# Moving the delta rule's constants, low-rank inputs and first tiles, and the first cache pages, into the stages before them

## The reference, cut to what matters

```python
def _attend_paged(q_lat, q_pe, c_kv, k_pe, cache_ckv, cache_kpe, layer, page_table):
    def page_step(carry, pages):                     # 64 pages of 128 rows for each sample
        kc = cache_ckv[layer, pages]
        kp = cache_kpe[layer, pages]
        return _online(carry, _scores(q_lat, q_pe, kc, kp), kc), None
    carry, _ = lax.scan(page_step, init, page_table.T)
    ...                                              # then the sample's own 4 rows, masked

prev = jnp.concatenate([shift0[:, None].astype(rw.dtype), rw[:, :-1]], axis=1)
xr = rw + (prev - rw) * lw["rwkv_mu"]                # token shift, all RWKV columns
r, k, v, xw, xa, xg = jnp.split(xr, RWKV_SPLITS, axis=-1)
w = -jax.nn.softplus(-(lw["rwkv_w0"] + jnp.tanh(xw) @ lw["rwkv_w_up"])) - 0.5
a = jax.nn.sigmoid(lw["rwkv_a0"] + xa @ lw["rwkv_a_up"])
g = jax.nn.sigmoid(xg) @ lw["rwkv_g_up"]
S = S * wt[:, :, None, :] + sa[..., None] * bt[:, :, None, :] + vt[..., None] * kt[:, :, None, :]
new_shift = rw[:, -1]
```

## Time and profile before

| | us |
|---|---|
| median of 3 runs | 3769.72 (3756.41 to 3772.3) |
| the profiled execution | 3773.11, span of its instructions 3771.3 |
| PE busy | 3410.2 (90% of the span) |
| DVE / ACT / POOL busy | 1652.5 / 941.2 / 396.7 |
| prompt attention, first instruction to end | 1435.3 to 1623.9 |
| opening of sample attention, up to the first page's transpose | 1623.9 to 1646.0 |
| sample attention after that | 1646.0 to 2050.6 |
| masks, then low-rank inputs | 2050.6 to 2059.9 to 2075.9 |
| delta rule | 2075.9 to 2510 |

### The profile page before, as it was taken

One profiled execution on the slowest core, in us unless ns is written; L12 is line 12 of the kernel. 1 busy time (PEld: TensorE's weight loads), 2 busy tenths in 40 slices (PEclk: granted clock), 3 DMA queues, 4 the chain that ended last, 5 costly groups with the idle time before them and its releaser, 6 DMA issues. The chain is left out here.

```text
span 3771.3 us, 69383 instructions
## 1 busy us (share of the span) xinstructions
PE 3410.2 (90%) x28749; PEld 3049.2 (81%) x28749; DVE 1652.5 (44%) x2947; ACT 941.2 (25%) x1651; POOL 396.7 (11%) x452
## 2 busy tenths in 40 slices
PE   7999999979999799979996788869979999999877
PEld 6999999978999736756664576659969999999866
DVE  3343344353222144435453677755154343343454
ACT  3111111122000104534442334433141111111231
POOL 0000000010000000033330334420010000000112
PEclk9999999989999898989997799979989999999988
DMA  2111111113222300045553201014031111111032
GB/s 104 34 56 46 34 51 51 40 64 119 90 92 94 118 14 10 9 167 203 195 192 91 51 25 32 20 64 148 29 131 51 51 40 44 51 40 46 32 132 99
DMA packets 118755, 279.39 MB, mean 74 GB/s; under 512 B 46036, under 2 KB 57108, under 8 KB 117940
## 3 DMA queue, kind: packets, MB, share of 16 engines
q1 hardware_dynamic: 100052, 199.87, 15.7%
q0 software_dynamic: 18432, 75.51, 5.8%
HBM read 231.41 MB, written 43.80 MB: 73 GB/s over the span
## 5 line engine op out<-in xcount | busy, mean ns | idle before, releaser
L79 PE MATMUL f_psg<-f_u_hi,f_w_hi 128*128 128x352 f32 x1056 | 349.3, 331 | 49.5 <-DVE f_u_lo L359 24.0
L590 DVE TENSOR_TENSOR c_x<-c_x,f_psd 128x352 f32<-128x352 f32 x480 | 246.6, 520 | 318.3 <-PE f_psd L81 318.3
L79 PE MATMUL f_psd<-f_hid_hi,f_w_hi 128*128 128x352 f32 x1056 | 350.5, 332 | 18.2 <-DVE c_x L590 9.8
L475 ACT ACTIVATE f_w_hi<-f_raw 128x1024 fp32r<-128x1024 f32 x132 | 136.8, 1054 | 916.9 <-PE f_psd L81 352.0
L80 PE MATMUL f_psg<-f_u_lo,f_w_hi 128*128 128x352 f32 x1056 | 344.2, 326 | 0.0
L81 PE MATMUL f_psg<-f_u_hi,f_w_lo 128*128 128x352 f32 x1056 | 344.1, 326 | 0.0
L80 PE MATMUL f_psd<-f_hid_lo,f_w_hi 128*128 128x352 f32 x1056 | 341.7, 324 | 0.0
L79 PE MATMUL f_psu<-f_u_hi,f_w_hi 128*128 128x352 f32 x1056 | 341.4, 323 | 0.0
L81 PE MATMUL f_psd<-f_hid_hi,f_w_lo 128*128 128x352 f32 x1056 | 341.4, 323 | 0.0
L80 PE MATMUL f_psu<-f_u_lo,f_w_hi 128*128 128x352 f32 x1056 | 339.4, 321 | 0.0
L81 PE MATMUL f_psu<-f_u_hi,f_w_lo 128*128 128x352 f32 x1056 | 339.0, 321 | 0.0
(11 more groups left out here) (403 smaller groups left out, 7051.1 us busy)
## 6 DMA issues: line engine op xcount, KB each, us to landing
f_raw<-in_ffn_gu SPq DMA_DIRECT2D x88, 512.0 KB, 4.2
f_raw<-in_ffn_d SPq DMA_DIRECT2D x44, 512.0 KB, 4.1
proj<-in_out SPq DMA_DIRECT2D x36, 528.0 KB, 2.9
inw_raw<-in_w_in_units SPq DMA_DIRECT2D x36, 512.0 KB, 3.9
h<-c_x SPq DMA_DIRECT2D x24, 528.0 KB, 2.9
c_x<-proj SPq DMA_DIRECT2D x16, 528.0 KB, 4.3
mgw_raw<-in_merge_units SPq DMA_DIRECT2D x16, 512.0 KB, 4.7
plw_raw<-in_ple_units SPq DMA_DIRECT2D x8, 640.0 KB, 3.9
```

Of the source, the lines that this page charges most:

```text
L79: pe.matmul(out, w_hi, x_hi, start=start, stop=False)
L475: act.activation(w_hi[:, u % 3, :], raw[:, u % 3, :], ACT.Copy).then_inc(hi_done, 1)
L590: dve.tensor_tensor(a, a, ps_d[:, n % 2, 0:TB], ALU.add).then_inc(added, 1)
```

## The change

Three things are moved, and the buffers are laid out anew for it.

1. A class `SamplePages` owns the table, the row numbers, `q_block`, `q` and the four slots of `pages`. Its loads (`sp_loads`), the four row-number instructions (`dve_rows`, after the fourth item's maximum) and the first sample's whole gather (`pool_prepare`, `pool_sequence(pool, 0, 0, None, None)`: 4 groups, 16 indirect DMAs) run in prompt attention. Sample attention starts with 5 constants instead of 10, `own_t` first, and three clears instead of four.
2. A class `RwkvInputs` owns `lw`, `lg`, `starts`, `lora`, `par`, `padded`. Once `weighted` has reached `2 * NS` in sample attention, SyncE issues all of `load_constants`, `lora_phase` and the first loads of `rwkv_phase` (`sp_loads`), in that order: low-rank inputs, last rows, masks, constants, first three tiles, and the store of the shift rows. VectorE mixes the low-rank inputs (`dve_mix`) between the scaling of `acc` and the copy of `o_lat`. ScalarE's tanh and sigmoid (`act_gates`) follow its last body.
3. The phases `load_constants` (masks) and `lora_phase` are gone. `rwkv_phase` starts with the state's load.

`q_t` and `k_t` lie in tiles of 128 partitions (`queries`, `keys`), whose room `RwkvInputs` uses later. `acc`, `weights` and `uv` of sample attention lie in the room of `v`. The instructions of the loops are the same.

```diff
+class SamplePages:
+    def sp_loads(self, sp):
+        sp.dma_start(self.table[:, :], self.page_table.broadcast_to([P, DEC_BATCH * N_PAGES])).then_inc(self.table_in, 16)
+        for m in range(self.QUAD):
+            sp.dma_start(self.row_no[m * self.ROWS:(m + 1) * self.ROWS, :], self.row_number[0:self.ROWS, :])\
+                .then_inc(self.table_in, 16)
+        sp.wait_ge(self.zeroed, 1)
+        for m in range(self.QUAD):
+            sp.dma_start(self.q_block[m * ROPE:(m + 1) * ROPE, :, m, :], self.q_pe[NOPE:QK, :, :])\
+                .then_inc(self.blocked, 16)
+    def dve_rows(self, dve):
+        dve.wait_ge(self.table_in, 16 * (self.QUAD + 1))
...
+    def pool_prepare(self, pool):
+        pool.memset(self.q_block[:, :, :, :], 0.0).then_inc(self.zeroed, 1)
+        pool.wait_ge(self.rows_at_ready, self.QUAD)
+        pool.wait_ge(self.blocked, 16 * self.QUAD)
...
 def prompt_attention_phase
             sp.dma_start(diag_mask[:, :], mask).then_inc(mask_in, 16)
+            sample.sp_loads(sp)
...
+                if n == 2:
+                    sample.dve_rows(dve)
...
+        @block.gpsimd
+        def _(pool):
+            sample.pool_prepare(pool)
+            sample.pool_sequence(pool, 0, 0, None, None)
...
 def sample_attention_phase
+        acc = spare[:, 0:4, :].rearrange("p a (m n) -> p (a m) n", n=KV_RANK)
+        weights = spare[:, 4:6, :].rearrange("p k (m n) -> p k m n", n=NQ)
+        uv = spare[:, 6:8, :]
...
-            sp.wait_ge(zeroed, 4)
-            sp.dma_start(own_rows[0:DEC_SEQ, :, :], new_rows.rearrange("b t n -> t b n")).then_inc(blocked, 16)
-            for m in range(QUAD):
-                sp.dma_start(q_block[m * ROPE:(m + 1) * ROPE, :, m, :], q_pe[NOPE:QK, :, :]).then_inc(blocked, 16)
+            sp.wait_ge(zeroed, 3)
+            sp.dma_start(own_rows[0:DEC_SEQ, :, :], new_rows.rearrange("b t n -> t b n")).then_inc(own_in, 16)
+            sp.wait_ge(weighted, 2 * NS)
+            early.sp_loads(sp)
             sp.wait_ge(head_out, 1)
...
+            sample.pool_sequence(pool, 0, 1, quad_scored, pages_free)
+            with pool.Fori(1, NB // 2) as i:
+                for k in range(2):
+                    sample.pool_sequence(pool, i, k, quad_scored, pages_free)
...
             stretches(act, body)
+            early.act_gates(act)
...
                               .broadcast_to([P, NB, KV_RANK]), ALU.mult).then_inc(scaled, 1)
+            early.dve_mix(dve)
             dve.wait_ge(lat_done, 1)
...
             pe.wait_ge(consts_in, 16 * N_CONSTS)
-            pe.wait_ge(blocked, 16 * (QUAD + 1))
+            pe.wait_ge(sample.blocked, 16 * QUAD)
+            pe.wait_ge(own_in, 16)
...
+class RwkvInputs:
+    def sp_loads(self, sp):
+        sp.dma_start(self.mu, self.mu_lora).then_inc(self.lora_in, 16)
+        for n in range(2):
+            load_padded(sp, self.lo_padded[:, n, :], self.proj, 12 + n, self.shift, self.lora_in)
+        sp.dma_start(self.last, self.proj[U_RW:U_RW + N_RW, :, SEQ - 1:T].rearrange("c p t -> p c t"))\
+            .then_inc(self.last_in, 16)
+        for out, src in self.masks:
+            sp.dma_start(out, src).then_inc(self.masks_in, 16)
...
+        sp.dma_start(self.starts, self.not_start).then_inc(self.consts_in, 16)
+        for i in range(3):
+            self.load_tiles(sp, i)
+        sp.wait_ge(self.last_in, 16)
+        sp.dma_start(self.new_shift, self.last).then_inc(self.last_out, 16)
+        sp.wait_ge(self.masks_in, 16 * len(self.masks))
+        sp.wait_ge(self.last_out, 16)
+    def dve_mix(self, dve):
+        for n in range(2):
+            dve.memset(self.lo_padded[:, n, 0:1], 0.0).then_inc(self.zeroed, 1)
+        dve.wait_ge(self.zeroed, 2)
+        dve.wait_ge(self.lora_in, 16 * 7)
+        for n, out in enumerate((self.lw, self.lg)):
+            shift_mix(None, dve, dve, self.lo_padded[:, n, :], self.diff, out, self.mu[:, n:n + 1],
+                      (self.diffed, self.mixed), n)
+    def act_gates(self, act):
+        act.wait_ge(self.mixed, 2)
+        act.activation(self.lw[0:64, :], self.lw[0:64, :], ACT.Tanh)
+        act.wait_ge(self.mixed, 4)
+        act.activation(self.lg, self.lg, ACT.Sigmoid)
```

More of the change, by code:

```diff
@@ L1441, in prompt_attention_phase @@
+def prompt_attention_phase(nc, env, q_t, k_t, v, mask, oa_dram, sample):
     H, NB = MLA_HEADS, SEQ // P
@@ L1620, in sample_attention_phase @@
     NS = GRP // QUAD
-    RING = 4
+    RING = sample.RING
     LOOP = 2 * NG
@@ L1635, in psum @@
             return ctx.enter_context(nc.psum_tensor(f"sa_{n}", shape, F32))
[L1637 to L1641, removed]
+        pages, q, q_block, q_ready = sample.pages, sample.q, sample.q_block, sample.q_ready
         own_rows = sb("own_rows", [P, NB, LAT])
@@ L1815, in _ @@
             dve.wait_ge(consts_in, 16 * N_CONSTS)
-            for m in range(QUAD):
-                r = slice(m * ROWS, (m + 1) * ROWS)
-                dve.tensor_scalar(rows_at[r, :], table[r, m:NB * N_PAGES:QUAD], float(ROWS), row_no[r, 0:1],
-                                  ALU.mult, ALU.add).then_inc(rows_at_ready, 1)
-            dve.wait_ge(zeroed, 4)
+            dve.wait_ge(zeroed, 3)
             dve.wait_ge(own_done, 1)
@@ L2106, in rwkv_phase @@
-def rwkv_phase(nc, env, masks, lw, lg, proj, shift, params, lora_w, not_start, state_in, yb_dram,
-               wkv_prompt, wkv_sample):
+            return kept.enter_context(nc.semaphore(f"ri_{n}"))
+        at = [0, T, 2 * T, 3 * T, 3 * T + 3 * RWKV_DIM, 3 * T + 3 * RWKV_DIM + 9 * self.PADDED]
+        self.lw, self.lg, self.starts = (region[:, at[n]:at[n + 1]] for n in range(3))
+        self.lora = region[:, at[3]:at[4]].rearrange("p (n d) -> p n d", n=3)
+        self.padded = region[:, at[4]:at[5]].rearrange("p (g n t) -> p g n t", g=3, n=3)
@@ new lines, in __init__, with work_in @@
+        self.par = ctx.enter_context(nc.sbuf_tensor("ri_par", [P, NPAIR, N_PAR], F32))
+        self.masks = masks
+        self.consts_in, self.masks_in = sem("consts_in"), sem("masks_in")
+        self.loaded = [sem(f"loaded{g}") for g in range(3)]
+        self.lora_in, self.zeroed, self.diffed, self.mixed = sem("lora_in"), sem("zeroed"), sem("diffed"), sem("mixed")
+        self.last_in, self.last_out = sem("last_in"), sem("last_out")
+    def work_in(self, spare, proj, shift, mu_lora, new_shift, lora_w, params, not_start):
+        n = 2 * (1 + SEQ + DEC_BATCH * 5)
+        self.lo_padded = spare[:, 0:n].rearrange("p (n t) -> p n t", n=2)
+        self.diff = spare[:, n:n + T]
+        self.last = spare[:, n + T:n + T + N_RW * (1 + T_DEC)].rearrange("p (c t) -> p c t", c=N_RW)
+        self.mu = spare[:, n + T + N_RW * (1 + T_DEC):n + T + N_RW * (1 + T_DEC) + 2]
+        self.proj, self.shift, self.mu_lora, self.new_shift = proj, shift, mu_lora, new_shift
+        self.lora_w, self.params, self.not_start = lora_w, params, not_start
@@ L2117, in rwkv_phase @@
+def rwkv_phase(nc, env, masks, early, proj, state_in, yb_dram, wkv_prompt, wkv_sample):
     LEVELS, GT, BANKS, HB = 4, 3, 7, P // 2
@@ L2886, in build @@
[L2886 to L2897 removed]
+                sample = SamplePages(nc, ctx, kept, env, q_lat, q_pe, a["cache"], a["table"], a["row_number"])
@@ L2900, in build @@
                      seeds[:, :, :], ident_half[:, :])
[L2901 to L2904 removed]
+            rwkv_phase(nc, env, masks, early, proj, a["state"], yb_dram, o["wkv_prompt"], o["wkv_sample"])
         with ExitStack() as ctx:
```

245 lines of the change are left out of this document (109 added, 136 removed).

## The result

| | before | changed |
|---|---|---|
| median of 5 runs each, us | 3769.72 (3756.41 to 3772.3) | 3731.25 (3726.0 to 3735.45) |
| ratio | | 0.9907, 95% interval 0.9894 to 0.9921 |
| profiled execution, its span | 3773.11, 3771.3 | 3733.34, 3731.6 |

The change gains 38.5 us by the medians and 39.8 by the profiled executions. The forecast was 3730.4.

The account below looks back on a forecast made before the run. TensorE is busy for 90% of the span, so gains must come where it stands still. 11.5 + 1.0 - 0.6 + 32.4 - 5 = 39.3 us off the profiled 3773.1, or 3730.4 against the median; range 3716 to 3750.

Parts of the forecast that it names:

- first handover: Prompt attention's end to the first page transpose: pages land early, only the own scores' chain stays; 11.5 us gained.
- clock of the first bodies: First bodies of sample attention: work without a break leaves less of them at low clock; 1 us gained, 0 to 2.5.
- prompt attention: Four row-number instructions on VectorE, 1.39 us, partly stick out of its idle 0.77 us; 0.6 us lost.
- second handover: Sample attention's end to the delta rule's scan: inputs already landed, mix hidden, scan sooner; 32.4 us gained, 31 to 33.5.
- loop: Sample attention's loop: SyncE's loads delay gathers of groups 5 to 7; 4 us of stalls, 1 of clock, 5 lost.
- the margin of 1.3 us for the mix: Second handover: VectorE's mix, 5.7 us, hidden beside 7.04 us of TensorE work, with 1.3 us to spare.
- the lower end: Loop: SyncE's packets alternate with a gather's; stalls of 1.4, 0.1 and 1.4 us, some 3 in all.
- fully hidden loads: Rival, loop of sample attention: SyncE's loads cost nothing, 44.3 us gained, 3725; chance 0.10.
- Loads served first: Rival, loop: SyncE's loads go ahead of gathers; 14 us of stalls and 3 of clock, 3742; chance 0.13.
- The late opening of the delta rule: Rival, second handover: something unseen, as code fetch, delays the opening; up to 12 of 32.4 us stay, 3742; chance 0.05.
- Slower gathers in every body: Rival, loop: gathers slower in all 28 groups; at 2.5 us each, 26 us slower than before, 3795; chance 0.04.
- the own scores hold TensorE: Rival, first handover: own scores or `consts_in` hold TensorE as before; gain shrinks to about 4 us, 3738; chance 0.05.

Follow-up runs that it names:

- part 1: Page table, row numbers, query blocks and first gather moved into prompt attention; with only this changed against the kernel before, 3750.6 us.
- part 2: Delta rule's loads, mix and gates moved into sample attention; with only this changed against the kernel before, 3733.2 us, ratio 0.9921.
- part 1 alone: Changed kernel with the delta rule's loads, mix and gates put back into a phase of their own behind sample attention: 3750.6 us, ratio 0.9965.
- the last kernel of the experiments: Changed kernel, loads at 29 groups, w_uv and same-query table issued behind own rows, own rows' wait behind own scores: 3721.9 us, again 3716.9.
- late kernel: Changed kernel with SyncE's gate at 29 groups' weighted sums instead of 2: 3716.4 us, ratio 0.9871; again 3719.4 us, 0.9878.
- the two portions: Changed kernel's loads split into large and small, one at gate 2, the other at 29: 3724.8 us with large at 2, 3723.3 with small.
- the burst: Changed kernel with only the large loads at the gate of 2, all at once, the small ones at 29: 3724.8 us, ratio 0.9879.
- the paced: Changed kernel with large loads at gates three groups apart, from 2 to 20, the small ones at 29: 3725.4 us, ratio 0.9894.
- the small loads: Changed kernel with only the small, strided loads at the gate of 2, the large ones at 29: 3723.3 us, ratio 0.9875.

## Why the prediction was right

The time was 0.9 us from the forecast by the median, and the mechanisms came as described. That it is so close is luck: the terms add up to 3 us less than was forecast, and stretches outside of the change made up for it.

| term, us | predicted | profile of the changed kernel | in the experiments |
|---|---|---|---|
| first handover | +11.5 (10.5 to 12.5) | +11.2 | 15.5 to 16.2 us long wherever part 1 is in and its waits are as they were |
| clock of the first bodies | +1 (0 to 2.5) | +0.2 | 29.8 to 30.3 from the first transpose to the request of group 4 wherever part 1 is in; 30.2 and 29.9 before |
| prompt attention | -0.6 (-3 to 0) | -0.5 | 183.8 to 184.1 with the rows' four instructions; 183.2 to 183.5 without |
| second handover | +32.4 (31 to 33.5) | +32.1 | 7.2 us long in all eleven profiles with part 2 |
| loop | -5 (-17 to -1) | -6.7 | changed, twice, against part 1 alone: -9.2 and -6.4; against the two profiles of before: -6.7 to -3.0 |
| sum | +39.3 | +36.3 | |

- First handover: the sum of its chain (issues, landing of the own rows, 4.3 us of own scores) gave 15.6 us and measured 16.0. That the own scores, not the pages, come last was right. What the prediction didn't see is that the own rows, w_uv and the same-query table, all of which it counted into the chain, could have been taken out of it: 4 us.
- Clock: this step failed in size. The prediction gave 1 us for pages at hand. The own scores ran at 1.2 GHz in both kernels (PEclk 0.50), and the clock came back 5.3 us behind the first transpose before, 4.8 in the changed kernel and 5.7 in the last kernel of the experiments; the 4 us of work without a break ahead of it gained nothing that stands out. The eight transposes take 1.97 us and took 1.94 in the earlier trace rows. Its bound of 0 held.
- Second handover: as forecast, but the margin of 1.3 us for the mix is thinner than it was counted. In the late kernel, where the clock is high when L2064 begins, that takes 5.17 us, less than the mix's 5.7, and TensorE then waits 1.17 us for the next copy, 0.78 in the changed kernel.
- Loop: the mechanism was right (groups a few bodies behind the gate are hit, a stall before one body spares the next, a stall of over 2 us costs clock besides), the size low. Stalls of 1.4, 0.1 and 1.4 us at the lower end, 4 taken in all; measured 2.73, 2.17 and 0.96, 5.9 in all. The engine time of the loads was about right: 23.0 us in the prediction, 10.6 and 10.2 for the two portions. Two things in the working fell short. It counted the loads' engine time in order of the list, at the rate seen in the phases of before; beside the gathers they took 54 us, not 40, and so touched more groups. And it set the size by which packets go first, while the burst, the paced and the small loads fit a size that hangs on how much is queued at once.
- The loop had also become faster by itself: 320.4 us with the early pages and no loads, against 322.8 and 323.7 before. With the other four profiles that have the early gather and no loads beside gathers it is 320.4 to 322.3, so 0.5 to 3.3 us of what the loads cost are hidden when the changed kernel is held against before. Why was not tried, and with two profiles of before it can be chance; 1.7 us of 323.7 are the stretch between groups 17 and 18 again.
- The rivals: fully hidden loads fell (5.9 us of waits). Loads served first would have cost 17 us and fell too. The prediction leaned to them by what the Trainium skill, "DMA: Bandwidth & Descriptors", section "Queues, rings and completion order", says of turns taken by packets of many descriptors; that many tiny descriptors then crowd out a gather was the prediction's own conclusion. It isn't borne out: the 15,104 packets of the small loads cost the loop 1.5 us, though SyncE's slow issuing spread them. For large ones the truth lies off the lower end: the gather beside the burst kept TensorE waiting 4.7 us, where loads served first would have delayed it by up to their 10.6 us, and equal shares of the engines by its own 6.9. The late opening of the delta rule fell: TensorE's first matmul there stands 3.9 us after VectorE's last copy, the scan 3.3 later. Slower gathers in every body fell (320.4 us). That the own scores hold TensorE since `uv` is among `consts_in` was half true: 4 us, but the own rows, on `own_in`, landed last.
- What isn't the prediction's merit: the stretches outside moved by +4.6, -5.0 and +3.8 us between the two profiles, and these add up to 3.4, which is what the sum of 36.3 lacks of the 39.8 between the profiles.

## What to carry to other kernels

Loads that are brought forward into a stretch with gathers in flight cost, as far as these profiles show, by how much engine time they queue at once, not by their bytes: put them behind the last gathers if what they feed is still hidden there, or spread them out (one per three bodies was tried here). Whether spreading saves time beyond the waits isn't shown, since the two kernels' times are alike. Before merging or moving phases, look at what ends them: here it was SyncE's issuing, 29.5 us, and only moving the issues away gained anything. In a wait for a set of loads, ask of each whether the instruction behind it reads it, and look which lands last: here the two constants and the own rows had to go together.

## What the runs showed of the hardware

- The longer stalls cost more than themselves. Waits of up to 1.95 us lengthened the interval between two requests by about as much or less (1.35 by 1.42, 1.80 by 1.29, 1.95 by 2.01), those from 2.17 us on by more (2.17 by 3.28, 2.73 by 4.25, 2.77 by 4.34, 3.03 by 3.88, 3.83 by 6.75, 4.69 by 7.15, each against the same interval of part 1 alone), with PEclk below 1 behind each of the latter and at 1.00 behind the former.
- The clock's fall in the tail of sample attention comes some 28 us after the request of group 31 in some executions and some 10 us later in others. (In the late kernel it fell at 28 us, came back 4 us later and fell again: 44.8 us.) It makes the tail 47.5 to 47.9 us or 43.6 to 45.0, with the same instructions; four of the fourteen profiles have the long one. What decides it stays open.
- The same loads took SyncE 54 us to issue among the gathers at the start of the loop, 50.7 in the middle of it, 29.6 behind the last ones and 29.5 with no gather near. That full DMA engines hold up the issuing is only a guess: it wasn't tried by itself, and in the late kernel the engines were 81% busy over the first 12 us of the loads without any delay.
